# Laying out a hybrid mixer anew: convolution taps from PSUM, another order of projections, tanh gates, output projection from the LRU half

## The reference, cut to what matters

```
z, xbc, dt_raw, xl, gate = split(rmsnorm(x) @ w_in)
# SSD half
xbc = silu(conv4(xbc)); xs, B, C = split(xbc)
dt = softplus(dt_raw + dt_bias); cum = cumsum(dt * A)
y = intra-chunk(C, B, exp(cum_t - cum_s), dt*xs) + inter-chunk(C, h) + D*xs
y_ssd = group_rmsnorm(y * silu(z))
# LRU half
xc = conv4(xl)
r = sigmoid(xc @ w_a + b_a); i = sigmoid(xc @ w_x + b_x)
log_a = -8 * r * softplus(-lam); a = exp(log_a)
u = sqrt(1 - exp(2*log_a)) * (i * xc);  h = scan(h*a + u)
y_lru = rmsnorm(h * gelu(gate))
x = x + concat(y_ssd, y_lru) @ w_out
```

## Time and profile before

| | us |
|---|---|
| median of 3 runs (1868.62 to 1874.81) | 1873.99 |
| the profiled execution, device time | 1870.91 |
| its span | 1869.2 |
| PE busy | 1757.8 (94%) |
| DVE busy | 1373.9 (73%) |
| ACT busy | 1033.0 (55%) |
| POOL busy | 174.3 (9%) |

### The profile page before, as it was taken

The page is one execution under the profiler, slowest core; times in us unless marked ns, Lnnn a source line. Parts: engine busy times, 40 slices in busy tenths (PEclk is TensorE's granted clock), DMA queues, the critical chain, the costliest instruction groups (busy, mean ns, idle before and its releaser), DMA issues.

```text
span 1869.2 us, 24016 instructions
## 1 busy us (share of the span) xinstructions
PE 1757.8 (94%) x9024; PEld 1462.9 (78%) x9024; DVE 1373.9 (73%) x1335; ACT 1033.0 (55%) x958; POOL 174.3 (9%) x167
## 2 busy tenths in 40 slices
PE   7999689999999978889999999999999999999996
PEld 6866578999887657878878878788788788787884
DVE  4755765554456586468888888888888888888885
ACT  2425244443222434346777677776767776776764
POOL 2026430000101553000000000000000000000000
PEclk9999889999999988989999999999999999999998
DMA  8425334555643452349999999899899999998991
GB/s 261 136 93 180 127 110 142 184 162 159 202 135 104 148 167 91 129 150 361 355 323 357 336 338 359 307 368 357 317 357 353 322 357 335 338 359 307 368 357 46
DMA packets 257026, 465.44 MB, mean 249 GB/s; under 512 B 8492, under 2 KB 108196, under 8 KB 256928
## 3 DMA queue, kind: packets, MB, share of 16 engines
q1 hardware_dynamic: 250288, 442.20, 68.5%
q0 software_dynamic: 6384, 21.28, 3.5%
q10 hardware_dynamic: 288, 1.08, 0.2%
HBM read 453.70 MB, written 11.15 MB: 249 GB/s over the span
## 4 chain that ended last, share of the span: by engine, by line
PE 82%; DVE 9%; ACT 3%; POOL 2%; issue 2%; DMA 1%; DVEq 0%; ACTq 0%; POOLq 0%
PE bank L811 80%; DVE arena L1516 3%; PE bank L815 3%; DVE arena L1519 1%; DMA arena<-in_state_ssd 1%; DVE w_lo L1519 1%; ACT arena L1237 1%; DVE moe_arena L1516 1%; POOL arena L697 1%; ACT L1237 1%; DVE arena L1736 1%; DVE fw_lo L1519 0%; ACT w_hi L1237 0%; POOL sam_tmp L697 0%; DVE rs L1519 0%
## 5 line engine op out<-in xcount | busy, mean ns | idle before, releaser
L1519 DVE TENSOR_TENSOR w_lo<-wring,w_hi 128x2048 fp32r<-128x2048 f32 x336 | 768.2, 2290 | 118.1 <-ACT w_hi L1237 117.2
L1237 ACT ACTIVATE w_hi<-wring 128x2048 fp32r<-128x2048 f32 x336 | 643.3, 1918 | 254.8 <-PE bank L811 254.7
L811 PE MATMUL bank<-w_hi,xg_hi 128*128 128x512 f32 x896 | 359.7, 401 | 10.6 <-DVE w_lo L1519 9.0
L811 PE MATMUL bank<-w_lo,xg_hi 128*128 128x512 f32 x896 | 355.1, 396 | 0.0
L811 PE MATMUL bank<-w_hi,xg_lo 128*128 128x512 f32 x896 | 352.7, 394 | 0.0
L811 PE MATMUL bank<-hn,wring 128*128 128x264 f32 x1152 | 270.4, 395 | 6.3 <-DVE hn L1516 6.1
L811 PEld LDWEIGHTS bank<-hn,wring 128*128 128x128 f32 x1152 | 221.4, 194 | 53.5 <-issue 13.1
L811 PEld LDWEIGHTS bank<-w_hi,xg_hi 128*128 128x128 f32 x896 | 168.3, 188 | 51.3 <-DVE w_lo L1519 12.6
L811 PEld LDWEIGHTS bank<-w_lo,xg_hi 128*128 128x128 f32 x896 | 168.2, 188 | 40.9
L811 PEld LDWEIGHTS bank<-w_hi,xg_lo 128*128 128x128 f32 x896 | 168.4, 188 | 38.6
L1519 DVE TENSOR_TENSOR fw_lo<-wring,fw_hi 128x2048 fp32r<-128x2048 f32 (+1 forms) x54 | 114.2, 2115 | 109.4 <-ACT fw_hi L1237 109.4
(11 more groups left out here) (239 smaller groups left out, 2201.8 us busy)
## 6 DMA issues: line engine op xcount, KB each, us to landing
wring<-in_moe_w_gate SPq DMA_DIRECT2D x112, 1024.0 KB, 5.2
wring<-in_moe_w_up SPq DMA_DIRECT2D x112, 1024.0 KB, 5.2
wring<-in_moe_w_down SPq DMA_DIRECT2D x112, 1024.0 KB, 5.0
wring<-in_w_in SPq DMA_DIRECT2D x36, 1024.0 KB, 5.3
wring<-in_w_out SPq DMA_DIRECT2D x16, 1024.0 KB, 5.7
wring<-in_ffn_w_gate SPq DMA_DIRECT2D x11, 1024.0 KB, 5.5
wring<-in_ffn_w_up SPq DMA_DIRECT2D x11, 1024.0 KB, 5.4
wring<-in_ffn_w_down SPq DMA_DIRECT2D x16, 704.0 KB, 4.8
```

The source lines that it names most:

```text
L811: return nc.tensor.matmul(out, lhsT, rhs, start=start, stop=stop)
L1237: return nc.scalar.activation(out, in_, fn, **kw)
L1519: return V.tensor_tensor(out, in0, in1, op)
```

## The change

- Convolutions: ScalarE no longer copies an `xbc` or `xl` tile. It writes the newest tap with its bias from PSUM straight into the result (`tap`), and keeps only 11 columns of the raw rows. VectorE adds the other three taps out of PSUM; the bank is released by its last instruction. Four banks in turn for `xbc`, three for `xl`.
- Order of TensorE: `dt` behind `xbc` tile 1, `scal` behind tile 9; `xtok`, `btok`, `cb`, `sin`, `state`, two `rows` behind `xl` tiles 1 to 6; then `gate` with `cum`, with `final` and `inter` behind tile 0 and two pairs of `ga`, `gx` behind each of tiles 0 to 3; then `z`, with `yT` behind tile 1, `hrows` behind 3, `lru_norm` behind 5, `ysam` behind 6.
- ScalarE: the LRU gates are Tanh of half the argument, the halves put into scales and constants; Gelu is one instruction over all of `gate`, Silu of `z` comes tile by tile.
- Sample states: three buffers; a step is `advance` q then the sum of q-1; one step at each of `gate` tiles 1, 3, 4, 6, 7 and 8 (past the last), step 0 in `xl`; the sum of chunk 7 far down in VectorE's list.
- `mix_lo` is made by VectorE instead of GpSimd.
- Output projection: eight units in the order `OUT_ORDER` (pair, 1 for LRU half): three LRU halves first; `ssd_norm` 0 and 1 stand before units 1 and 2; `out` tiles use six banks in turn, so tiles 6 and 7 reuse the banks of tiles 0 and 1.

The diff, cut to its core (moved helper bodies, bank plan and memory layout left out):

```diff
-STEPS_AT_Z = {1: (0, 1), 2: (2,), 3: (3,), 5: (4,), 7: (5,)}
+CONV_BANKS = {"xbc": (BA, BB, Q1, Q2), "xl": (BA, BB, BN)}
+OUT_BANKS = (BA, BB, Q1, Q2, Q3, Q4)
+OUT_ORDER = ((0, 1), (1, 1), (2, 1), (0, 0), (3, 1), (1, 0), (2, 0), (3, 0))
+DT_AT = 1
+SCAL_AT = 9
+INTRA_AT = 1
+HROWS_AT = 3
+YSAM_AT = 6
+LRU_NORM_AT = 5
+STEPS_AT_GATE = {1: 1, 3: 2, 4: 3, 6: 4, 7: 5, 8: 6}
...
+STATE_BUFS = 3
...
+def gates_at(m):
+    return (2 * m, 2 * m + 1) if m < XT // 2 else ()
...
                 state_term(l, 0)
+                b, n = fill("state", l, NC - 1, GROUPS - 1)
+                pool.wait_ge(full[b], n + 1)
+                load_states(l, 2)
+                state_out(l, 0)
...
+                state_term(l, 1)
+                for q in range(2, STATE_CHUNKS):
                     state_term(l, q)
                     state_out(l, q - 1)
...
-                for half, src in enumerate((ygl, ysz)):
-                    for i in range(XT):
-                        k = XT * (1 - half) + i
-                        pool.wait_ge(mix_hi_ready, 16 * l + XT * half + i + 1)
-                        nc.gpsimd.tensor_tensor(mix_lo[:, k], src[:, i, :], mix_hi[:, k].bitcast(F32), ALU.subtract
-                                                ).then_inc(mix_lo_ready, 1)
...
+                for i in range(2, 5):
+                    conv_rows(l, i)
                 for m in range(XT):
-                    project(("z", l, m), l, m, "z", lambda k: hn[:, k], KD)
...
+                    for mt in gates_at(m):
+                        evacuated("xl", l, mt)
+                        for i, kind in enumerate(("ga", "gx")):
+                            out = begin(kind, l, mt)
+                            done(mm(out[:, 0:T], gate_w[:, i, mt, :], xlc[:, mt, :]), kind, l, mt)
...
+                        out = begin("ysam", l)
+                        pe.wait_ge(sum_ready, STATE_CHUNKS * (l + 1))
...
+                    if m == LRU_NORM_AT:
+                        mean_square(("lru_norm", l), mean_d[:, :], [th[:, i] for i in range(XT)],
+                                    lambda i: pe.wait_ge(lsq_ready, 2 * l + 1 + (i >= LRU_EARLY)))
...
+                for q, (pair, lru) in enumerate(OUT_ORDER):
+                    if 1 <= q <= GROUPS:
+                        ssd_norm(q - 1)
+                    for m in (2 * pair, 2 * pair + 1):
+                        out = begin("out", l, m) if lru else bank[fill("out", l, m)[0]]
+                        first = m == 0
+                        ins = split_product(
+                            out, OUT[l][q], XT * (1 - lru), 2 * XT, mix_hi, mix_lo, m % 2 * P,
+                            (lambda k: pe.wait_ge(mix_hi_ready, 16 * l + k + 1)) if first else None,
+                            (lambda k: pe.wait_ge(mix_lo_ready, 16 * l + k + 1)) if first else None)
+                        if not lru:
+                            done(ins, "out", l, m)
+                    if lru:
+                        ins.then_inc(half_used, 1)
                 mean_square(("ln_ffn", l), mean_d[:, :], [sq[:, m] for m in range(KD)],
...
+                def tap(kind, m, rows, dst, w, b):
+                    out = filled(kind, l, m)
+                    f(rows[:, m, :], out[:, TP - 3:T])
+                    f(dst[:, m, 0:TP], out[:, 0:TP], ACT.Identity, scale=w, bias=b).then_inc(tap_ready, 1)
                 for m in range(XBC + 1):
                     if m < XBC:
-                        evacd(f(raw[:, m, 3:], filled("xbc", l, m)[:, 0:T]), "xbc", l, m)
+                        tap("xbc", m, raw, xc, col(l, PA, "conv_w", 3 * XBC + m), col(l, PA, "conv_b", m))
                     if m > 0:
-                        act.wait_ge(conv_ready, 22 * l + m)
+                        evacuated("xbc", l, m - 1)
                         f(xc[:, m - 1, 0:TP], xc[:, m - 1, 0:TP], ACT.Silu).then_inc(xc_ready, 1)
...
+                        evacd(f(ygl[:, m, :], filled("gate", l, m)[:, 0:T]), "gate", l, m)
...
+                    for mt in gates_at(m):
+                        evacd(f(rg[:, mt, :], filled("ga", l, mt)[:, 0:T], ACT.Tanh, scale=0.5, bias=col(l, PA, "b_a", mt)),
+                              "ga", l, mt)
+                        evacd(f(ig[:, mt, :], filled("gx", l, mt)[:, 0:T], ACT.Tanh, scale=0.5, bias=col(l, PA, "b_x", mt)),
+                              "gx", l, mt)
                     if m > 0:
                         evacuated("cum", l, m - 1)
                         f(seg[:, 2 * m - 2:2 * m], seg[:, 2 * m - 2:2 * m], ACT.Exp).then_inc(segexp_ready, 1)
...
+                act.wait_ge(mult_arg, l + 1)
+                f(th[:, :, :], th[:, :, :], ACT.Sqrt, scale=0.25).then_inc(mult_ready, 1)
                 for i in range(2):
-                    evacuated("z", l, XT - 1 - i)
-                f(ysz[:, :, :], ysz[:, :, :], ACT.Silu).then_inc(z_ready, 1)
+                    evacuated("gate", l, XT - 1 - i)
...
+                act.wait_ge(seg_done, 8 * (l + 1))
                 for m in range(XT):
-                    evacd(f(ygl[:, m, :], filled("gate", l, m)[:, 0:T], ACT.Gelu_apprx_tanh), "gate", l, m)
-                    if m == INTRA_AT:
-                        act.wait_ge(mult_arg, l + 1)
-                        f(th[:, :, :], th[:, :, :], ACT.Sqrt).then_inc(mult_ready, 1)
+                    evacd(f(ysz[:, m, :], filled("z", l, m)[:, 0:T], ACT.Silu), "z", l, m)
...
+                        act.wait_ge(st_stored[2], 16 * (l + 1) * chunks_of(2))
+                        high_weights(OUT[l][1])
...
+                    if m == 4:
+                        for i, (m0, m1_) in enumerate(((0, LRU_EARLY), (LRU_EARLY, XT))):
+                            act.wait_ge(ylru_ready, 2 * l + i + 1)
+                            f(th[:, m0:m1_, :], ygl[:, m0:m1_, :], ACT.Square).then_inc(lsq_ready, 1)
+                    if m == LRU_NORM_AT:
+                        rms(("lru_norm", l), 2)
+                    if m == 6:
+                        high_parts(1, 0, XT)
...
+                ssd_squares(0)
+                rms(("ssd_norm", l, 0), 0)
+                ssd_squares(1)
+                high_parts(0, 0, 4)
+                rms(("ssd_norm", l, 1), 1)
                 for q, j in enumerate(OUT[l]):
-                    if q % 2:
-                        for m in (q - 1, q):
+                    pair, lru = OUT_ORDER[q]
+                    def out_squares():
+                        for m in (2 * pair, 2 * pair + 1):
                             evacuated("out", l, m)
                             f(sq[:, m], xT[:, m], ACT.Square).then_inc(sq_ready, 1)
+                    if q == len(OUT[l]) - 1:
+                        out_squares()
                     if j + FSLOTS < len(SPLIT):
                         unit_used(act, j)
                         high_weights(j + FSLOTS)
+                    if not lru and q < len(OUT[l]) - 1:
+                        out_squares()
+                    if q == 0:
+                        high_parts(0, 4, XT)
...
+            def conv(l, kind, dst, table, w, tiles, m):
+                taps = XBC if kind == "xl" else 0
+                dve.wait_ge(tap_ready, (XBC + XT) * l + taps + m + 1)
+                out = bank[fill(kind, l, m)[0]]
+                for d in range(1, CW):
+                    v = dst[:, m, d:TP]
+                    ins = stt(v, out[:, 0:TP - d], col(l, table, w, (CW - 1 - d) * tiles + m), v)
+                    if d < CW - 1:
                         link(ins)
-                ins.then_inc(conv_ready, 1)
+                evacd(ins, kind, l, m)
...
-                if q >= 2:
-                    sum_state(l, q - 2)
-                if q < STATE_CHUNKS:
-                    advance(l, q)
+                advance(l, q)
+                if q:
+                    sum_state(l, q - 1)
...
+                    if m in STEPS_AT_GATE:
+                        step_state(l, STEPS_AT_GATE[m])
+                    if m == 5:
+                        evacuated("gx", l, XT - 1)
+                        ins = stt(ig[:, :, :], ig[:, :, :], 1.0, xlc[:, :, :], ALU.add, ALU.mult)
                         dve.wait_ge(lru_exp, XT * (l + 1))
+                        link(ins)
...
-                link(tt(ig[:, :, :], ig[:, :, :], xlc[:, :, :], ALU.mult))
-                step_state(l, 6)
                 dve.wait_ge(mult_ready, l + 1)
-                link(V.memset(th[:, :, 0:1], 1.0))
...
-                for q in range(8, STATE_CHUNKS + 2):
-                    step_state(l, q)
-                for i in range(4):
-                    evacuated("yT", l, i)
-                dve.wait_ge(z_ready, l + 1)
-                tt(ysz[:, :, 0:TP], ysz[:, :, 0:TP], xc[:, 0:XT, 0:TP], ALU.mult).then_inc(yssd_ready, 1)
...
+                dve.wait_ge(gelu_ready, l + 1)
...
+                for m0, m1_ in ((0, LRU_EARLY), (LRU_EARLY, XT)):
+                    tt(ygl[:, m0:m1_, :], ygl[:, m0:m1_, :], th[:, m0:m1_, :], ALU.mult).then_inc(ylru_ready, 1)
                 low_weights(OUT[l][0])
```

(52 more changed lines are left out.)

730 lines of the change are left out of this document (361 added, 369 removed).

## The result

The changed kernel takes 1894.3 us in the median of 4 runs (1889.95 to 1895.52), beside 1872.1 for the kernel before (4 runs): a ratio of 1.011, with a 95% interval of 1.0094 to 1.0126. It is slower by 22 us, where 1868 was predicted with 1892 as the upper end. On another chip it took 1894.5 (ratio 1.0118, 1.0103 to 1.0134). The kernel before had medians of 1869.8 to 1873.3 on the chips of this study, so a gain read from medians of two chips is uncertain by some 3 us.

What follows compares the result with a forecast made beforehand. VectorE's list, stretched by GpSimd's chunks, was taken to bound the mixer's second half. Per layer 3.4 us gained in front less 1.8 lost after gave 3.4 in all off 1870.91: 1867.5, stated as 1868, range 1840 to 1892.

Steps and rivals of the forecast that it cites:

- the five waits: PE's waits before the last `yT` 5.3, `hrows` 9.8, `ysam` 8.1, unit 2 4.8 and unit 4 4.8 us, each layer.
- Front part: From `xbc` to the start of `gate`: small products between `xl` tiles find inputs ready, waits go; gain 3.4 us.
- The cost of the taps: `xbc` and `xl` convolutions: VectorE's three instructions read PSUM, about 0.4 us each; nothing waits while VectorE keeps up.
- Gates: LRU gate products as two pairs behind each of four tiles: 7.8 us instead of 11.6, gain 3.8 us.
- `gate` stage: From `gate`'s first tile: VectorE's list, with scans at 4.8 us, frees the bank of `yT` 1 at 85.0 us.
- The rule that was weighed: Ports go to whichever of VectorE and GpSimd starts first: `ig` 2.3 us, not 4.8, total 1863; prediction charged the loss.
- The sum: 181.7 us from `gate` against 179.9, 1.8 lost, 3.4 gained in front: 3.4 us in all off 1870.91, giving 1867.5.
- Rival 2: VectorE's list from `gate` tile 4 to `yT` 1 later than counted, 9 us a layer: 1886, chance 0.25.
- taps at 1.1 us: Instructions reading PSUM behind ScalarE's tap cost 1.1 us; PE waits for `xl` banks, 6 us a layer: 1880, chance 0.03.

Runs made afterwards that it cites:

- the moves of the sum: Changed kernel with the sum of state chunk 7 ahead of the LRU norm instead of behind its low parts and a weight unit: 1876.7 us.
- of the add: Changed kernel with VectorE's residual add of each finished output tile ahead of the next unit's low weights: 1880.7 us.
- of unit 2: Changed kernel with ScalarE making output unit 2's high weights before the root of the second SSD norm: 1891.2 us.
- the Sigmoid form: Changed kernel with the LRU gates by Sigmoid again, with their scales and constants, everything else in place: 1899.7 us.
- The kernel with both causes removed: Changed kernel with `cb` in another bank, GpSimd's last chunk held until the LRU scans end, and step 7 with chunk 6's sum behind the LRU product: 1867.3 us.
- step 7's move: Changed kernel with step 7 and the sum of chunk 6 behind the LRU product, GpSimd not held back; alone 1892.8 us.
- five small moves: Changed kernel with chunk 7's sum early, residual add first, `cb` in another bank, state steps earlier and unit 2's high weights early: 1830.2 us, 0.9782.

## Why the prediction was wrong

**What bounds the kernel, and the five waits: right, one length by luck.** All five came where they were put, within 0.3 us but for `hrows`. So did their reasons, as the moves of the sum, of the add and of unit 2 show; in unit 2 the reason was half right: ScalarE's list held it, and VectorE's norm stood behind. That the last `yT` waits 5.31 us, for 5.3, is luck: PE comes to it at t = 63.1 instead of 61 and is released at 68.4 instead of 66.3. The first is a misreading of the old timeline, where three `yT` products take 6.0 us as they do now (178.18 to 184.18), 2.0 each and not 1.5 (PE, kernel before; the first and the last line of the three):

```profile
178.94 0.39 PE L811 MATMUL bank<-ident,arena 128*128 128x128 f32 x2
...
184.28 0.66 PE L811 MATMUL bank<-arena 128*64 128x128 f32 x8
```

It cost nothing, since PE waits for VectorE in front of `hrows` either way.

**Front part, "gain 3.4 us": the step that failed first.** "Between `xl` tiles the small ones find their inputs ready" looked at inputs and not at banks. `btok`, `cb`, `sin` and two `rows` follow each other through Q0, each waits for the reader of the one before it, and that reader's list now has a tap or a convolution in front. It cost 1.21 + 2.88 us and 1.7 to 1.8 of slow clock: 2.4 lost instead of 3.4 gained. With `cb` in another bank the front part takes 90.1 us and gains 3.8, so the rest of that step was right. The order of the fills stood in the plan; it was not walked through for this stretch. The cost of the taps was rightly put at nothing, and `rows` 3 and 4 wait 0.75 us for the 1.1 that was counted.

**Gates: half right.** The pairs between the tiles cost the wait of ScalarE as predicted (0.22 us), and the pitch of a gate tile with its `cum` and pairs is 7.05 us instead of 6.76. That ScalarE's table loads are hidden holds for the tanh form; the Sigmoid form pays 3 to 5 us here.

**`gate` stage, "scans 4.8": the step that failed second.** The price was that of a row in which GpSimd was idle. The prediction's own times end step 6 at 73.3. That is when `ig` times `th` starts, with the scans from 76.2 to 81, and it is also when the sum of chunk 5 is done and GpSimd may begin chunk 7, some 7 us of work: the meeting was in the sum for `ig` times `th` and was left out for the scans. Measured 9.71, 4.95 us more a layer. Another 2.7 had come before: `ig` times `th` starts at t = 76.0 instead of 73.3 (and the last `yT` at 68.4 instead of 66.3). The pitch of the tiles is a small part of it (VectorE takes up `cum` 4 at 35.6 instead of 35). The rest is VectorE instructions other than the updates and `ig`, which the sum had at full speed and which met GpSimd too: `seg` products of 1.57 and 1.58 us, and one of 3.35 at 157.67, where 0.7 was counted, and 1.86 for 0.98 in the root's argument. Together with 0.5 us too much for `ig` times `th` this makes up the 7.0 us by which `hrows` starts late; from there to the last add it is 96.5 us, and 96.7 was predicted.

**The rule that was weighed.** By "whoever starts first holds the ports", `ig` would have taken 2.3 us. It began at 166.27, ahead of GpSimd's L742 at 166.37, and took 4.68, as the prediction charged. But `ig` times `th`, ahead of L733 by 0.02 us, took its full-speed 2.36, and GpSimd's instruction 4.09 instead of 1.89: there the rule holds, and the prediction's 2.9 was too much by 0.5. One thing sets the cases apart in the rows: `ig`, and the update that took 3.99 us from 191.13 on, began while GpSimd was issuing a store (L740 from 165.75 and from 191.05); `ig` times `th` began with GpSimd idle. All 12 slow updates of the kernel before began 0.07 to 0.08 us behind such an issue too. No run tests whether the issue is the cause. The Trainium skill says in the same section of "SBUF — State Buffer", "Who interferes with whom", that a VectorE instruction with two inputs in SBUF contends with a GpSimd instruction that reads SBUF. A scan here has two. The prediction weighed the sentence about who wins and passed over the one about who takes part; the scans agree with that one, at 9.71 us beside GpSimd and 4.76 without.

**The sum.** 1867.5 with 5.8 a layer for the front part and 4.95 for the scans is 1889, and the 2 us a layer that are left of the rest of VectorE's list make 1893. The kernel with both causes removed took 1867.3. That it is the time of the forecast is in part luck: step 7's move is in it too, and hides the 2 us a layer of VectorE's list.

**Rivals.** Rival 2 was the side that came true, in its stretch (VectorE's list between `gate` tile 4 and `yT` 1 was 7.0 us later than counted), but what it priced was two more meetings of updates and one more slow stretch, not the scans and the small instructions, and its price ended at 1886. Nothing in the rivals stood for the front part but taps at 1.1 us. Two independent misses of the same sign, each of about 10 us, are what took the time past 1892.

## What to carry to other kernels

When work is reordered, walk through each shared buffer as well as each engine: for every fill of a bank, ask in which place of the reader's new list its predecessor is read. Where a sum charges a contention to some instructions of a stretch, charge it to all that have the same operands, and take no price from a row in which the other engine was idle. And a slower new order isn't a wrong one: the same reordering with five small moves went from 1.1% slower to 2.2% faster.

## What the runs showed of the hardware

- A VectorE scan with both inputs in SBUF all but stands while GpSimd works: 8 scans took 9.71 us with 5.6 us of GpSimd's instructions beside them, 4.76 without, so that they got through 0.7 us of their work in those 5.6.
- The order of starting decides only sometimes who loses: VectorE's `ig` began 0.10 us ahead of GpSimd and lost 2.3 us; `ig` times `th` began 0.02 ahead and lost nothing; an update that began 0.54 ahead took 3.99 us instead of 1.28 (191.13 against L742 at 191.67 in the changed kernel). In the rows the losers began while GpSimd was issuing a store and the winner did not; no run tests it, so what tells them apart stays open.
- An activation whose bias is a column, beside its scale, took 595 ns instead of 500. The Trainium skill, "ScalarE: Activation LUTs", "What ACT_TABLE_LOAD costs", gives about 93 ns for each such operand; the trace agrees.
- What a wait of PE costs in clock afterwards isn't fixed: behind the same 2.87 us `xl` 5 took 5.52 us in one execution and 3.83 in another, and behind the same 7.85 us `z` 7 took 5.37 us in one kernel and 6.74 in another (granted clock 0.71 and 0.56). So differences of 1 to 2 us between single profiles can be the clock's.
- A table load took 1.28 us and nothing more: in the Sigmoid kernel the load at 138.41 is followed by an exponential at 139.70.
